# Softmax divided before the turn: attention with its values' product transposed and moved, in two of four layers of a kernel

## The reference, cut to what matters

```python
def one_block(qs):
    s = None
    for qp, kp in zip(qs, k_parts):          # MLA: a part of 128 and one of 64; GQA: one part of 128
        t = jnp.einsum(eq, qp, kp)
        s = t if s is None else s + t
    p = jax.nn.softmax(s * scale, axis=-1)
    return jnp.einsum('bkgqs,bskd->bqkgd', p, v)
...
mem_out = _memory_attention(q_mem, mem_n, w_mem_kv[i], memq_norm[i], memk_norm[i])   # the same, 4 heads of 128
x = x + jnp.concatenate([mix, mem_out], axis=-1) @ w_out[i]
```

## Time and profile before

| | |
|---|---|
| median of 3 runs | 1251.92 us (1251.01 to 1252.02) |
| the profiled execution | 1250.17 us, span of its records 1248.4 us |
| TensorE matmuls (PE) | 1234.9 us busy, 99% of the span |
| VectorE (DVE) | 812.5 us, 65% |
| ScalarE (ACT) | 667.7 us, 53% |
| GpSimd (POOL) | 89.9 us, 7% |
| HBM | 173 GB/s over the span |

### The profile page before, as it was taken

How to read it: one execution, slowest core, us unless ns; L and a number is a source line. 1 busy time by engine, 2 the same in 40 slices (tenths; PEclk the granted TensorE clock), 3 DMA queues, 4 the chain that set the end, 5 groups by cost and what they waited for, 6 DMA issues and landing times.

```text
span 1248.4 us, 15778 instructions
## 1 busy us (share of the span) xinstructions
PE 1234.9 (99%) x6366; PEld 1029.9 (83%) x6366; DVE 812.5 (65%) x1036; ACT 667.7 (53%) x965; POOL 89.9 (7%) x121
## 2 busy tenths in 40 slices
PE   7999999999999999999999999999999999999998
PEld 6778888888888888888888888888888888888887
DVE  7995756644788766554687746656547775656553
ACT  7765654433898654443687535443436644544431
POOL 2510000000100100000233000000001200000000
PEclk9999999999999999999999999999999999999999
DMA  8343555555554565545554134655555315555551
GB/s 306 109 144 136 195 192 174 197 179 192 192 201 168 187 225 175 200 171 202 184 193 169 68 106 164 205 198 172 192 187 182 124 42 206 192 195 176 192 180 66
DMA packets 32392, 216.60 MB, mean 174 GB/s; under 512 B 3888, under 2 KB 4272, under 8 KB 7232
## 3 DMA queue, kind: packets, MB, share of 16 engines
q1 hardware_dynamic: 30240, 210.19, 48.7%
q0 software_dynamic: 1360, 4.78, 1.2%
q10 hardware_dynamic: 720, 0.63, 0.2%
HBM read 214.54 MB, written 1.05 MB: 173 GB/s over the span
## 4 chain that ended last, share of the span: by engine, by line
PE 93%; DVE 4%; issue 1%; DMA 1%; ACT 0%; SPq 0%; DVEq 0%; ACTq 0%
PE PS L461 26%; PE PS L463 26%; PE PS L462 26%; PE PS L467 6%; PE PS L775 2%; PE PS L799 1%; PE PS L498 1%; PE PS L496 1%; PE PS L495 1%; PE PS L544 1%; PE PS L538 1%; PE PS L539 1%; DVE WL L1731 1%; DVE YG L2013 1%; DMA X<-in_x 1%
## 5 line engine op out<-in xcount | busy, mean ns | idle before, releaser
L1731 DVE TENSOR_TENSOR WL<-RAW,WH 128x2048 fp32r<-128x2048 f32 (+2 forms) x200 | 442.6, 2217 | 310.5 <-ACT WH L1114 310.5
L1114 ACT ACTIVATE WH<-RAW 128x2048 fp32r<-128x2048 f32 (+2 forms) x200 | 371.0, 1858 | 366.2 <-PE PS L463 366.1
L461 PE MATMUL PS<-WH,HTh 128*128 128x512 f32 (+1 forms) x848 | 334.6, 395 | 1.2 <-DVE WL L1731 1.0
L463 PE MATMUL PS<-WH,HTl 128*128 128x512 f32 (+1 forms) x848 | 329.0, 388 | 0.0
L462 PE MATMUL PS<-WL,HTh 128*128 128x512 f32 (+1 forms) x848 | 328.3, 387 | 0.0
L463 PEld LDWEIGHTS PS<-WH,HTl 128*128 128x128 f32 x848 | 159.2, 188 | 33.3
L461 PEld LDWEIGHTS PS<-WH,HTh 128*128 128x128 f32 x848 | 159.3, 188 | 33.1 <-DVE WL L1731 2.1
L462 PEld LDWEIGHTS PS<-WL,HTh 128*128 128x128 f32 x848 | 159.5, 188 | 30.6
L461 PE MATMUL PS<-WH,YAh 128*128 128x512 f32 x402 | 158.6, 394 | 0.1
L463 PE MATMUL PS<-WH,YAl 128*128 128x512 f32 x402 | 156.7, 390 | 0.0
L462 PE MATMUL PS<-WL,YAh 128*128 128x512 f32 x402 | 156.5, 389 | 0.0
(11 more groups left out here) (352 smaller groups left out, 1441.6 us busy)
## 6 DMA issues: line engine op xcount, KB each, us to landing
RAW<-in_w SPq DMA_DIRECT2D x196, 1024.0 KB, 4.9
BC<-in_rows POOLq DMA_DIRECT2D x4, 512.0 KB, 4.1
YG<-in_mem POOLq DMA_DIRECT2D x4, 512.0 KB, 4.5
X<-in_x SPq DMA_DIRECT2D x2, 512.0 KB, 5.4
RAW<-in_w SPq DMA_DIRECT2D x4, 256.0 KB, 5.4
BC<-in_s SPq DMA_DIRECT2D x1, 512.0 KB, 11.4
YG<-in_s SPq DMA_DIRECT2D x1, 512.0 KB, 11.8
BB<-in_s SPq DMA_DIRECT2D x1, 512.0 KB, 12.4
```

Of the source, the lines that this page charges most:

```text
L461: e.matmul(out, ah, bh, start=start, stop=False)
L463: return e.matmul(out, al, bh, start=False, stop=stop)
L1114: e.activation(WH[:, c % NW, w], RAW[:, c % NR, w], ACT.Copy).then_inc(S.hi, 1)
L1731: e.tensor_tensor(WL[:, c % NW, w], RAW[:, c % NR, w], WH[:, c % NW, w].bitcast(f32), SUB).then_inc(S.lo, 1)
```

## The change

It alters the attention of these two mixers and nothing else.

- The softmax is divided before the turn. VectorE's `share(h)` takes the reciprocal of one head's sums (128x2), one head ahead of the copy, and GpSimd's `norm` multiplies P of that head (128x512) with it in place. `turn_p(h)` waits for that (`S.pn`) and no more for the exps.
- The values' product is transposed: the values are the stationary operand and PT moves, 256 columns at a time, so the result has the features on its partitions. Two heads share a bank. The divided result needs no turn: `group_divide`, `Y` and `finish` are gone, and ScalarE's `attn_group` copies out of the product's own banks.
- On TensorE `pv(h - 1)` stands ahead of `turn_p(h)`, and `fill(h)` ahead of both where h > 3.
- On GpSimd the GQA mixer's root g3 stands between the divisions of heads 3 and 4.

```diff
@@ TensorE
-                    for t in range(2):
-                        e.wait_ge(S.ex, 2 * (base + h) + t + 1)
+                    e.wait_ge(S.pn, base - 8 + h + 1)
+                    for t in range(2):
                         for kt in range(2):
                             tk = transp(...)
...
-                    for t in range(2):
-                        b, o = heads[h]["banks"][t], heads[h]["at"]
-                        for kt in range(2):
-                            tk = e.matmul(PS[:, b, o:o + 128], PT[:, h % 2, kt, 128 * t:128 * t + 128], heads[h]["v"][kt],
-                                          start=kt == 0, stop=kt == 1)
+                    b, o = heads[h]["banks"][h % 4 // 2], 256 * (h % 2)
+                    for kt in range(2):
+                        tk = e.matmul(PS[:, b, o:o + 256], heads[h]["v"][kt], PT[:, h % 2, kt, :], start=kt == 0, stop=kt == 1)
                     tk.then_inc(S.pv, 1)
...
                     for h in range(13):
                         if h + 2 < 12:
                             products(h + 2)
+                        if h > 3:
+                            fill(h)
+                        if h:
+                            pv(h - 1)
                         if h < 12:
                             turn_p(h)
-                        fill(h)
-                        if h:
-                            pv(h - 1)
-                        if h in (5, 9):
-                            finish(h - 5)
+                        if h <= 3:
+                            fill(h)
@@ ScalarE
                 for jp in range(2):
-                    attn_out(2 + 2 * ((base - 8) // 4 + g) + jp + 1, heads[4 * g]["banks"][jp], at + 2 * jp)
+                    e.wait_ge(S.pv, base + 4 * g + 2 * jp + 2)
+                    copy(YAh[:, at + 2 * jp:at + 2 * jp + 2, :], pair(heads[4 * g]["banks"][jp])).then_inc(S.oh, 1)
@@ VectorE
+                def share(h):
+                    e.wait_ge(S.ex, 2 * (base + h) + 2)
+                    e.reciprocal(den[:, :, h:h + 1], den[:, :, h:h + 1]).then_inc(S.rd, 1)
...
                 top(0)
                 top(1)
-                for h in range(13):
+                share(0)
+                for h in range(12):
                     if h + 2 < 12:
                         top(h + 2)
+                    if h < 11:
+                        share(h + 1)
...
                     fill(h)
-                    if h % 4 == 0 and h:
-                        group_divide(h // 4 - 1)
-                    elif h in (6, 10):
+                    if h in (6, 10):
                         group_lo(h // 4 - 1)
@@ GpSimd
+            def norm(base, P, den, hs):
+                for h in hs:
+                    e.wait_ge(S.rd, base - 8 + h + 1)
+                    e.tensor_tensor(P[:, h % 2, :, :], P[:, h % 2, :, :], den[:, :, h:h + 1].to_broadcast([128, 2, 256]), MUL).then_inc(S.pn, 1)
...
             head_rsqrt("nk1", 8)
+            norm(8, P2, den2, range(12))
...
             head_rsqrt("g1", 8)
+            norm(20, P3, den3, range(4))
             head_rsqrt("g3", 8)
+            norm(20, P3, den3, range(4, 12))
```

More of the change, by code:

```diff
@@ L228 @@
     w0a w0b w0c w0d hi1 lo1 pa pd pg pp rt rtz dv ev pairs uq rope ropes bhalf bu ang sab trig nr bread bet bbe k0p k0 ch w ssm gy gh gl
-    qk mx ex tp pta ptd pv yt ytp oh ol glua glud
+    qk mx ex rd pn tp pta ptd pv yt ytp oh ol glua glud
     lama lamd zo zt xg conv cph cpl gt tg odth odaa b4 b1 b2 b3 b8 b9 b10
@@ L764, in attention0, with attention_ahead @@
                 return finish
-            def attention_ahead(base, heads, P, PT, Y, ready, fill, pvfree, tfree=None):
+            def attention_ahead(base, heads, P, PT, ready, fill, pvfree, tfree=None):
                 def products(h):
@@ L795, in pv @@
                         e.wait_ge(S.ol, 2 + 2 * ((base - 8) // 4) + 2)
-                    for t in range(2):
-                        b, o = heads[h]["banks"][t], heads[h]["at"]
-                        for kt in range(2):
-                            tk = e.matmul(PS[:, b, o:o + 128], PT[:, h % 2, kt, 128 * t:128 * t + 128], heads[h]["v"][kt],
-                                          start=kt == 0, stop=kt == 1)
-                    tk.then_inc(S.pv, 1)
[L803 to L807, removed]
+                    b, o = heads[h]["banks"][h % 4 // 2], 256 * (h % 2)
+                    for kt in range(2):
+                        tk = e.matmul(PS[:, b, o:o + 256], heads[h]["v"][kt], PT[:, h % 2, kt, :], start=kt == 0, stop=kt == 1)
+                    tk.then_inc(S.pv, 1)
                 def attend():
@@ L812, in attend @@
                             products(h + 2)
+                        if h > 3:
+                            fill(h)
+                        if h:
+                            pv(h - 1)
                         if h < 12:
                             turn_p(h)
-                        fill(h)
-                        if h:
-                            pv(h - 1)
-                        if h in (5, 9):
-                            finish(h - 5)
-                return products, attend, finish
+                        if h <= 3:
+                            fill(h)
+                return products, attend
             def gain_turn(src, name, bks, free=None, tiles=4):
@@ L1047, in pe @@
             CQ, CK = (CTh, CTl), (CTh[:, 3:5, :], CTl[:, 3:5, :])
-            products2, attend2, finish2 = attention_ahead(8, HEADS2, P2, PT2, Y2, ready2, fill2, pvfree2, tfree2)
+            products2, attend2 = attention_ahead(8, HEADS2, P2, PT2, ready2, fill2, pvfree2, tfree2)
             edge_mm(PLAN["mla_a"], 4, 448, (0, 1), 4)
@@ L1067, in pe @@
             attend2()
-            wide_mm(PLAN["out0"], 5, lambda k: (YAh, YAl, OUT0[k // 2] + k % 2), lambda ci: e.wait_ge(S.ol, 3 + ci), lambda: finish2(8))
+            wide_mm(PLAN["out0"], 5, lambda k: (YAh, YAl, OUT0[k // 2] + k % 2), lambda ci: e.wait_ge(S.ol, 3 + ci))
             ffn(2, 5)
@@ L1097, in pvfree3 @@
                     e.wait_ge(S.gout, GT["g3"] + 2)
-            products3, attend3, finish3 = attention_ahead(20, HEADS3, P3, PT3, Y3, ready3, fill3, pvfree3)
+            products3, attend3 = attention_ahead(20, HEADS3, P3, PT3, ready3, fill3, pvfree3)
             edge_mm(PLAN["gqa0"], 4, 512, (0, 1), 6)
@@ L1105, in pe @@
             attend3()
-            wide_mm(PLAN["out1"], 7, lambda k: (YAh, YAl, k), lambda ci: e.wait_ge(S.ol, 9 + ci), lambda: finish3(8))
+            wide_mm(PLAN["out1"], 7, lambda k: (YAh, YAl, k), lambda ci: e.wait_ge(S.ol, 9 + ci))
             ffn(3, 7)
@@ L2288, in dve, with attention_ahead @@
             two = lambda Z: [Z[:, t, :] for t in range(2)]
-            def attention_ahead(base, heads, M, den, PT, Y, fill, at):
+            def attention_ahead(base, heads, M, den, PT, fill, at):
                 def top(h):
@@ L2376, in fill2 @@
                     feed(PLAN["kvb1"][0])
-            last2 = attention_ahead(8, HEADS2, M2, den2, PT2, Y2, fill2, (0, 8, 4))
+            last2 = attention_ahead(8, HEADS2, M2, den2, PT2, fill2, (0, 8, 4))
             wide_mm(PLAN["out0"], 5, last2)
@@ L2422, in fill3 @@
                     feed(PLAN["gqa1"][1])
-            last3 = attention_ahead(20, HEADS3, M3, den3, PT3, Y3, fill3, (0, 4, 8))
+            last3 = attention_ahead(20, HEADS3, M3, den3, PT3, fill3, (0, 4, 8))
             feed(PLAN["gqa3"][0])
```

## The result

The changed kernel takes **1257.05 us** (median of 4 runs, 1256.79 to 1257.17), the kernel before 1251.47 on the same chip (1250.59 to 1252.02). The ratio is 1.0048, 95% interval 1.0037 to 1.006: slower by 5.6 us, 0.45%. The profiled executions stand further apart, 1257.02 against 1250.17, because that of the kernel before is faster than all four of its runs here; their spans are 1255.2 and 1248.4, 6.8 us apart.

A forecast was written before the change was run, and what follows sets the result against it. TensorE, 99% busy, was the bound. Stepping the engines' orders (the walk) gave 16.4 us of new waits less 3.3 (old waits), 5.2 and 0.7: +7.1, laid on the 1251.92 median as 1259.0 us; range 1255 to 1264.

The forecast's parts named there:

- Taken away: TensorE in both mixers: group transposes of the divided result gone, 5.2 us; value products in 4 passes, not 8, 0.7 us.
- Item 1: Last three heads of each mixer: no score product covers turn, copy and load; TensorE stands 1.03 us each, 6.2 us.
- Item 2: Five heads with a one-part score product: 0.86 us covers all but 0.17 of the copy wait; 0.9 us.
- Item 3: Copies behind VectorE's weights splits: waits at MLA heads 2 and 4, GQA heads 7 and 8; 4.9 us.
- Item 4: GQA gain turns: 1.15 us at score product 4, 1.8 us for VectorE's g3 scaling; 2.9 us stated net.
- Item 5: Mixer entries: first MLA turn behind the first division, 0.5 us, first value products behind the copy, 0.6 and 0.5; 1.6 us.
- Reciprocal 0.15: Each of 24 new reciprocals taken to hold VectorE's queue 0.15 us; at 0.31 the sum would be +7.9 us.
- VectorE waits as well: VectorE's splits and g3 scaling start up to 0.9 us late beside GpSimd divisions; included in +7.1 us, without it +5.6.
- TensorE's count alone: Rival: on 99% busy TensorE only the 5.2 + 0.7 us removed counts, giving 1246.0 us; chance 0.05.
- Only tail, entry and short waits: Rival: queues slide so VectorE-queue and gain-turn waits vanish; 8.7 us against 9.2, about 1251.4 us; chance 0.07.
- GpSimd the bound: Rival: at 1.6 us a division, turns wait for GpSimd; +11.4 us, 1263.3 us; chance 0.13.
- The lower clock: Rival: pauses over each mixer's last three heads drop TensorE's clock; +7.8 us more, 1266.8 us; chance 0.08.

The follow-up runs named there:

- e1: Changed kernel with TensorE's order of the last two turns of each mixer put back, turns of heads 10 and 11 ahead of the previous value product: 1254.16 us.
- e2: Changed kernel with TensorE's order of the kernel before throughout (turn, fill, value product); GpSimd division and transposed product stay: 1250.84 us, kernel before 1250.55.
- e4: Changed kernel with VectorE's four weights splits moved, MLA from heads 1, 3, 7 to 4, 7, 11, GQA from head 7 to 9: 1254.99 us.
- e7: Changed kernel with the gain turn at head 4 put back behind turn 4, ahead of the next score product: 1256.06 us.
- e5: Changed kernel with TensorE's order of the kernel before, and VectorE dividing each head in two products instead of GpSimd: 1254.27 us, kernel before 1250.76.
- e3: Changed kernel with GpSimd doing each GQA head's product twice, the first into a buffer nobody reads: 1263.49 us, kernel before 1250.55.
- e9: e10 with weights splits moved too (MLA heads 4, 7, 11; GQA halves at heads 7 and 9): 1247.25 us, ratio 0.9969 to the kernel before.
- e10: e2 with VectorE taking the reciprocal of head h + 1 ahead of the maximum of head h + 2: 1248.89 us, kernel before 1250.94.

## Why the prediction was right, and where it was off

The direction, the mechanism and the range (1255 to 1264) held. Step by step:

- **Taken away, 5.2 + 0.7.** No transposes of a divided result are left. Of the tail's 2.35 a head, 1.31 are left without the wait and its charge of 1.04: 0.44 for the turn and 0.87 for four passes, where eight took 0.89.
- **How the items are compared.** The prediction counts by starts: what lies between two starts beyond the 0.87, 0.44 or 0.11 that the piece holds the queue at full pace. The idle time that the view gives for a load is another measure: where a score product stands in front it reads 0.32 for a delay of 0.17 by starts. The values below are by starts.
- **Item 1, tail, 6 x 1.03.** Six times 1.04 (the loads' idle time is 1.02). Right to a hundredth; e1 and e2 confirm its cause.
- **Item 2, one-part heads, 0.17 each.** The step from 1012.89 to 1015.24 is 2.35 us, its three pieces are 0.87 + 0.44 + 0.87 = 2.18: 0.17. Five loads have the 0.32 us before them that goes with it (698.34, 1005.62, 1012.89, 1015.24, 1017.59), the five heads of the prediction. Right, and not tested apart.
- **Item 3, behind VectorE's queue, 1.7, 0.7, 0.4, 2.0.** By starts 1.6, 0.6, 0.3 and 1.8 (idle before the loads: 1.75, 0.74, 0.42, 1.91). That is 4.2, where the prediction has 4.9 (its four numbers add up to 4.8): the one item that was too large. e4 confirms the cause.
- **Item 4, gain turns, 1.15 and 1.8.** 1.19 and 1.86. e7 gets 1.12 of it back.
- **Item 5, entries, 1.6.** The first turn of the MLA mixer starts at 693.32, 0.5 us late, released by the division; the first value products are 0.6 (MLA, 696.01) and 0.4 (GQA, 999.05) late. 1.5 in all, read from the trace and not tested by a run.
- **The sum.** By starts the new waits are 15.9 us against 16.4; less 9.2 they give 6.7, and the windows 6.9. The recorded terms, rounded, add up to 16.5 and 7.3, not 16.4 and 7.1.
- **Division 1.05.** 1.04, all 24. The nearest row was the same operation with the same kind of input, and it was the right one to take.
- **Reciprocal 0.15.** Its record lasts 0.16, but the next instruction starts 0.07 behind it (1019.25 to 1019.32). This term was twice too large; with 0.07 the walk falls from 7.1 to 6.8, and each head behind a split in item 3 has one such reciprocal in its way.
- **VectorE waits as well.** The 7.1 had it in, 5.6 was the sum without it. The split of 2.77 and the scaling of 1.93 for two (1.28 before) decide for the first; the difference at these two places is 0.5 + 0.65 us. In e5, where GpSimd divides nothing, the two take 2.28 and 1.28 again, so the division is the cause. (The 5.6 between the medians is no sign for the other sum; see *the level*.) The Trainium skill (SBUF — State Buffer, section "SBUF: two separate sides") calls it an exclusive lock that whoever starts first keeps; both directions are in rows here, the second in e3.
- **The stretches.** Forecast 37.9 and 35.6 to the projection's first product; they are 37.67 (691.08 to 728.75) and 35.24 (996.58 to 1031.82).
- **The level.** The one step that failed in size is the last: +7.1 was laid on the median of the runs shown, 1251.92, which gave 1259.0. The measured difference between medians is 5.6, and between profiled executions 6.85. The sum was made against an execution at 1250.17, and its own level, 1257.3, is within 0.3 of the result. The kernel before scatters by 1.4 us, the changed one by 0.4.

**The rivals.** *TensorE's count alone*: the work is gone (5.9 us by the prediction's count, 6.0 by the busy time of e9), and 15.9 us of new waits stand against it. *Only tail, entry and short waits*: items 3 and 4 are there. *GpSimd the bound*: TensorE waits for a division once in 24 turns, at the MLA mixer's entry. In e3, at 2.1 us a head, a plain step still takes 2.35 us and only some places wait for GpSimd, so in that order the bound of a plain step is not reached at 2.1. In the old order GpSimd's chain is on the path (e2), mostly through its reciprocal (e10). *The lower clock*: in the changed kernel it is granted in full (1.00 in both windows), with a pause of 1 us in every 2.35, six times. e3 shows that it exists in this kernel, after a stand of 2.05 and 1.12 us with one transpose between. The rows that the rival rested on the earlier trace rows show a pace and no more: the windows view gives a granted clock of 1.00 from 8 to 11 us, so why a matmul came only every 0.43 us there stays open. The Trainium skill (TensorE: Matmul & The Clock Gate, section "A second HAM failure mode: psum-queue depth-cycling") is borne out by e3 in so far as pauses inside a stage can bring the clock down; the tail of the changed kernel shows that pauses of a microsecond with 1.3 us of work between did not.

Left open: items 2 and 5 were not tested apart, the 1.8 us of e3's slow stretch is an estimate, and what of e9 the exclusion of GpSimd and VectorE costs was not tried. Its trace shows how little is left: every split there takes its plain 2.28 us (1.21 a half), and only the scaling of g3 is still long, 2.12 for 1.28.

## What to carry to other kernels

When a product is moved ahead of the step that used to cover its own input's copy, count the chain turn, copy, load at each place, the last heads above all: a pipeline needs its cover in the tail too. Before an order is changed to give a slow step more time, look at what that step itself waits for; here it was a 0.07 us reciprocal behind a 0.6 us maximum and a 2.3 us split, and moving it was worth 2.7 us, where moving the product and the gain turns cost 6.1. Lay a sum worked out against one profiled execution on that execution's own time, or say how far the median of a kernel that scatters may be from it.

## What the runs showed of the hardware that I had not expected

- A division on GpSimd beside VectorE's split is 1.04 us when it is first, and then it is VectorE that pays (2.77 for 2.28, in the changed kernel, e2 and e3); the other way round GpSimd takes 3.09 (e3). In e10, where the reciprocal comes first, the GQA split is clear of the division and takes 2.28 again.
- VectorE's reciprocal of 128x2 has a record of 0.16 us and costs 0.07 of the queue (1019.25 to 1019.32); where the next instruction waits for its result through a semaphore, it is 0.20 (e5, 708.00 to 708.20).
- In these stretches TensorE's clock fell to 0.50 once, in one of the ten variants (e3, in its profiled execution), and was back 3 us later; the 40 slices of that kernel's page do not show it.
